# Inverse roots of the model-wide norms: square root on ScalarE and reciprocal on VectorE, in place of exp of minus half the logarithm

## What is computed

```python
def rmsnorm(x, g):
    xf = x.astype(jnp.float32)
    y = xf * lax.rsqrt(jnp.mean(xf * xf, axis=-1, keepdims=True) + EPS)
    return (y * g.astype(jnp.float32)).astype(x.dtype)

def trunk(x, c, g_norm, w_ada, b_ada, g_final, even_p, odd_p):
    for l in range(DEPTH):
        mod = jax.nn.silu(c) @ w_ada[l] + b_ada[l]
        shift, scale, gate = jnp.split(mod, 3, axis=-1)
        h = rmsnorm(x, g_norm[l]) * (1 + scale[:, None, :]) + shift[:, None, :]
        ...
        x = x + gate[:, None, :] * out
    return rmsnorm(x, g_final)
```

## Time and profile before

| | |
|---|---|
| median of 3 runs | 1512.5 us |
| lowest and highest run | 1511.76 and 1519.93 us |
| the profiled execution's own time | 1513.49 us |
| its span on the core | 1511.7 us |
| mean granted clock of TensorE | 0.995 |
| busy share PE / DVE / ACT / POOL | 97% / 56% / 45% / 24% |

### The profile page before, as it was taken

One profiled execution on the slowest core, in us unless ns is written; L12 is line 12 of the kernel. 1 busy time (PEld: TensorE's weight loads), 2 busy tenths in 40 slices (PEclk: granted clock), 3 DMA queues, 4 the chain that ended last, 5 costly groups with the idle time before them and its releaser, 6 DMA issues.

```text
span 1511.7 us, 18941 instructions
## 1 busy us (share of the span) xinstructions
PE 1463.7 (97%) x7188; PEld 1117.8 (74%) x7188; DVE 852.8 (56%) x1523; ACT 678.3 (45%) x1170; POOL 355.3 (24%) x448
## 2 busy tenths in 40 slices
PE   8999999999999999999999999999999999999996
PEld 5677765678777787878887886567867778787885
DVE  7523345755885527884443345575588651789423
ACT  3323446645433435543543344674443353555233
POOL 2011023431200023755110002342120002376311
PEclk9999999999999999999999999999999999999999
DMA  9566732224332331116234443221432333111531
GB/s 382 200 214 215 256 117 85 64 56 132 102 94 84 126 104 49 43 48 230 86 127 130 126 125 98 84 57 57 140 98 86 96 113 115 52 42 31 181 97 69
DMA packets 54618, 174.27 MB, mean 115 GB/s; under 512 B 6000, under 2 KB 7408, under 8 KB 52224
## 3 DMA queue, kind: packets, MB, share of 16 engines
q1 hardware_dynamic: 54528, 173.07, 35.7%
HBM read 149.94 MB, written 23.10 MB: 114 GB/s over the span
## 4 chain that ended last, share of the span: by engine, by line
PE 81%; DVE 8%; ACT 5%; DMA 3%; issue 2%; POOL 1%; SPq 0%; DVEq 0%; ACTq 0%; POOLq 0%
PE ps L553 21%; PE ps L554 21%; PE ps L555 21%; PE ps L1095 4%; PE ps L1130 2%; PE ps L1149 2%; PE ps L1618 1%; PE ps L1601 1%; DMA at<-w_ada 1%; DVE w_lo L535 1%; PE ps L302 1%; PE ps L1652 1%; PE ps L1441 1%; PE ps L1112 1%; DMA at<-z_kept 1%
## 5 line engine op out<-in xcount | busy, mean ns | idle before, releaser
L535 DVE TENSOR_TENSOR w_lo<-at,w_hi 128x1024 fp32r<-128x1024 f32 x160 | 199.0, 1244 | 355.2 <-ACT w_hi L523 355.2
L523 ACT ACTIVATE w_hi<-at 128x1024 fp32r<-128x1024 f32 x162 | 169.4, 1046 | 122.6 <-PE ps L555 121.1
L553 PE MATMUL ps<-h_e_hi,w_hi 128*128 128x512 f32 x480 | 190.8, 398 | 7.8 <-DVE w_lo L535 7.8
L555 PE MATMUL ps<-h_e_hi,w_lo 128*128 128x512 f32 x480 | 187.1, 390 | 0.0
L554 PE MATMUL ps<-h_e_lo,w_hi 128*128 128x512 f32 x480 | 186.9, 389 | 0.0
L553 PE MATMUL ps<-h_a_hi,w_hi 128*128 128x512 f32 x384 | 153.6, 400 | 1.8 <-DVE h_a_lo L585 1.0
L554 PE MATMUL ps<-h_a_lo,w_hi 128*128 128x512 f32 x384 | 150.2, 391 | 0.0
L555 PE MATMUL ps<-h_a_hi,w_lo 128*128 128x512 f32 x384 | 150.1, 391 | 0.0
L553 PEld LDWEIGHTS ps<-h_e_hi,w_hi 128*128 128x128 f32 x480 | 90.0, 188 | 43.7 <-DVE at L1427 11.7
L555 PEld LDWEIGHTS ps<-h_e_hi,w_lo 128*128 128x128 f32 x480 | 90.1, 188 | 19.3
L554 PEld LDWEIGHTS ps<-h_e_lo,w_hi 128*128 128x128 f32 x480 | 90.2, 188 | 18.3 <-issue 0.5
(11 more groups left out here) (289 smaller groups left out, 2972.8 us busy)
## 6 DMA issues: line engine op xcount, KB each, us to landing
at<-blocks_in SPq DMA_DIRECT2D x162, 512.0 KB, 3.7
at<-w_ada SPq DMA_DIRECT2D x32, 512.0 KB, 4.6
at<-w_ada SPq DMA_DIRECT2D x8, 1024.0 KB, 18.1
at<-xs SPq DMA_DIRECT2D x4, 2048.0 KB, 10.5
z_kept<-at SPq DMA_DIRECT2D x32, 256.0 KB, 2.2
at<-z_kept SPq DMA_DIRECT2D x32, 256.0 KB, 2.9
sg_kept<-at SPq DMA_DIRECT2D x16, 256.0 KB, 4.5
at<-sg_kept SPq DMA_DIRECT2D x16, 256.0 KB, 2.7
```

The source lines that it names most:

```text
L523: act.activation(whi[:, n % PAIRS, :, cols], wring[:, n % SLOTS, :, cols], ACT.Copy).then_inc(sem("w_hi"), 1)
L535: dve.tensor_tensor(wlo[:, n % PAIRS], wring[:, n % SLOTS], whi[:, n % PAIRS].bitcast(F32), ALU.subtract)\
L553: pe.matmul(o, stationary[0], moving[0], start=first, stop=False)
L555: return pe.matmul(o, stationary[1], moving[0], start=False, stop=final)
```

## The change

At all six places the Ln becomes a Sqrt with the same scale and bias, and the Exp is dropped. The tile then holds the root. A RECIPROCAL on DVE, in place on the same 128x512 tile, takes the Exp's part and raises the semaphore that Exp raised. The early table load asks for Sqrt's table.

```diff
         def n_rstd(act, bank):
 
-            act.preload_act_table(ACT.Ln)
+            act.preload_act_table(ACT.Sqrt)
             act.wait_ge(sem("nx_ms"), at("nx_ms", 1))
-            act.activation(rstd, ps(bank), ACT.Ln, bias=cst("eps"), scale=1.0 / D).then_inc(sem("nx_ln"), 1)
-            act.wait_ge(sem("nx_ln"), at("nx_ln", 1))
-            act.activation(rstd, rstd, ACT.Exp, scale=-0.5).then_inc(sem("rstd_done"), 1)
+            act.activation(rstd, ps(bank), ACT.Sqrt, bias=cst("eps"), scale=1.0 / D).then_inc(sem("nx_ln"), 1)
+
+        def n_inverse(dve):
+
+            dve.wait_ge(sem("nx_ln"), at("nx_ln", 1))
+            dve.reciprocal(rstd, rstd).then_inc(sem("rstd_done"), 1)
...
         def fin_scale(dve, j):
 
+            if j == 0:
+                dve.wait_ge(sem("fin_ms"), at("fin_ms", 1))
+                dve.reciprocal(y_rstd, y_rstd).then_inc(sem("fin_rs"), 1)
             dve.wait_ge(sem("fin_rs"), at("fin_rs", 1))
...
         def dve_up(dve):
             dve.wait_ge(sem("shl"), at("shl", 1))
+            dve.wait_ge(sem("ln_done"), at("ln_done", 1))
+            dve.reciprocal(rstd, rstd).then_inc(sem("rstd_done"), 1)
             dve.wait_ge(sem("rstd_done"), at("rstd_done", 2))
```

More of the change, by code:

```diff
@@ L74 @@
 Group = namedtuple("Group", "a_sync a_gpsimd a_tensor a_scalar a_vector e_sync e_gpsimd e_tensor e_scalar e_vector act_split dve_split stream_weights"
-                           " dve_h act_h n_square n_gpsimd n_tensor n_rstd fin_tensor fin_rstd fin_scale fin_out")
+                           " dve_h act_h n_square n_gpsimd n_tensor n_rstd n_inverse fin_tensor fin_rstd fin_scale fin_out")
 def out1_block(b):
@@ L454, in p_vector @@
         dve.wait_ge(sem("mod_set"), 3)
+        groups[0].n_inverse(dve)
         dve.wait_ge(sem("rstd_done"), 1)
@@ L663, in fin_rstd @@
         def fin_rstd(act, bank):
-            act.preload_act_table(ACT.Ln)
+            act.preload_act_table(ACT.Sqrt)
             act.wait_ge(sem("ms_full"), at("ms_full", 2))
-            act.activation(y_rstd, ps(bank), ACT.Ln, bias=cst("eps"), scale=1.0 / D).then_inc(sem("fin_ms"), 1)
-            act.wait_ge(sem("fin_ms"), at("fin_ms", 1))
-            act.activation(y_rstd, y_rstd, ACT.Exp, scale=-0.5).then_inc(sem("fin_rs"), 1)
+            act.activation(y_rstd, ps(bank), ACT.Sqrt, bias=cst("eps"), scale=1.0 / D).then_inc(sem("fin_ms"), 1)
         def fin_scale(dve, j):
+            if j == 0:
+                dve.wait_ge(sem("fin_ms"), at("fin_ms", 1))
+                dve.reciprocal(y_rstd, y_rstd).then_inc(sem("fin_rs"), 1)
             dve.wait_ge(sem("fin_rs"), at("fin_rs", 1))
@@ L1381, in act_up @@
         def act_up(act):
-            act.preload_act_table(ACT.Ln)
+            act.preload_act_table(ACT.Sqrt)
             act.wait_ge(sem("ms_full"), at("ms_full", 1))
-            act.activation(rstd, ps(MS_BANK), ACT.Ln, bias=cst("eps"), scale=1.0 / D).then_inc(sem("ln_done"), 1)
-            act.wait_ge(sem("ln_done"), at("ln_done", 1))
-            act.activation(rstd, rstd, ACT.Exp, scale=-0.5).then_inc(sem("rstd_done"), 1)
+            act.activation(rstd, ps(MS_BANK), ACT.Sqrt, bias=cst("eps"), scale=1.0 / D).then_inc(sem("ln_done"), 1)
             act_h(act, 1, 1, h_E, range(2))
@@ L2029, in e_vector @@
                     if n == N_AT + 3:
+                        groups[g + 1].n_inverse(dve)
                         dve.wait_ge(sem("rstd_done"), 2 * (g + 1) + 1)
@@ L2039, in group @@
         return Group(a_sync, a_gpsimd, a_tensor, a_scalar, a_vector, e_sync, e_gpsimd, e_tensor, e_scalar, e_vector, act_split, dve_split,
-                     stream_weights, dve_h, act_h, n_square, n_gpsimd, n_tensor, n_rstd, fin_tensor, fin_rstd, fin_scale, fin_out)
+                     stream_weights, dve_h, act_h, n_square, n_gpsimd, n_tensor, n_rstd, n_inverse, fin_tensor, fin_rstd, fin_scale, fin_out)
     groups.extend(group(g) for g in range(G))
```

## The result

| | before | after |
|---|---|---|
| median of 11 runs | 1513.13 us | 1527.82 us |
| lowest and highest | 1510.34 and 1521.68 us | 1519.84 and 1531.89 us |
| the profiled execution's own time | 1513.49 us | 1529.53 us |
| its span, mean granted clock | 1511.7 us, 0.995 | 1527.7 us, 0.985 |
| busy us of DVE / ACT | 852.8 / 678.3 | 872.5 / 667.3 |

The account below looks back on a forecast made before the run. The prediction held that what counts is whether PE, or the program's end, waits for the inverse root. From 1512.5 us it added 7.7 (3.38 + 3 x 1.44) and 1.7 for TensorE's clock: 1521.9 us, range 1517.0 to 1530.0.

Parts of the forecast that it names:

- What the Exp's part costs: Between Ln's end and DVE's first step: 2.05 us in layer 1, 1.97 at the end, as load, Exp and handover.
- The reciprocal, 3.35 us: Each 128x512 reciprocal on DVE takes 3.35 us, extended from pairs of narrow ones in the same setting.
- Start-up +3.38: Start-up: the reciprocal and a handover of 0.03 us are all new, since Exp and load were hidden; +3.38 us.
- Layer 1 +1.44 each: Layer 1, both groups: reciprocal and handovers take 3.49 us in place of 2.05, +1.44 us each.
- The end +1.44: End of the program: reciprocal and handovers take 3.41 us in place of 1.97, +1.44 us.
- Hidden places, 0: First group's last projection and second group's first projection: PE never stops there, so the change costs 0.
- The clock, +1.7: Layer 1, both groups: TensorE's granted clock falls behind the longer waits, 0.85 us each, +1.7 us.
- the rival in which the clock holds: Layer 1: no added clock fall, the sum without that term, +7.7 us or 1520.2 us; chance 0.25.
- Start-up clock, "no change there": Start-up: the granted clock falls already behind PE's stop, so no change was counted there.
- A longer reciprocal: Rival, every place: reciprocal takes 4.3 to 5.5 us, sum 11.5 to 16.3 us, total 1525 to 1533.3 us; chance 0.17.
- a plain pass: Rival, every place: the wide reciprocal takes only 0.67 us, sum -3.0 us, total 1509.5 us; chance 0.08.
- slack in layer 1: Rival: layer 1 has unseen slack, so only start-up and end count, +4.8 us, 1517.3 us; chance 0.08.

Follow-up runs that it names:

- e1_start: Sqrt and reciprocal only at the start-up's norm of the first group, otherwise the kernel before; ratio 1.0021 (0.9994 to 1.0048).
- e3_end: Sqrt and reciprocal only at the second group's final norm, at the very end, otherwise the kernel before; ratio 1.0001 (0.9973 to 1.0029).
- e4_hidden: Sqrt and reciprocal only at the second group's first norm and the first group's final norm, otherwise the kernel before; ratio 1.0003 (0.9978 to 1.0027).
- e8_start_fill: e1_start with nine filler matmuls on TensorE in the 4.4 us wait for the first h_lo; 1520.78 us, ratio 1.0032 to the kernel before.
- e2_layer1: Sqrt and reciprocal only at the two norms of layer 1, otherwise the kernel before; ratio 1.0029 (1.0002 to 1.0055).
- e5_one_table: Kernel before, Ln and Exp kept, early load naming the table set that holds both; 1508.68 us against 1519.19, ratio 0.9964.
- e6: Kernel before with seven filler matmuls on TensorE in the start-up phase; 1521.74 us, ratio 1.0014 (0.9990 to 1.0038).
- e7: e5_one_table with seven filler matmuls on TensorE in the start-up phase; 1518.13 us, ratio 0.9995 to the kernel before.

## Why the prediction was right, and where it was off

- **What bounds the kernel.** Right. ACT is rid of 11 us (678.3 to 667.3) and DVE does 20 us more, and neither number tells anything of the 8.3 us lost; the four places where PE or the end waits for the root tell it.
- **What the Exp's part costs.** Right: 0.69 us for the Sqrt and handovers of 0.03 to 0.1 us, as in the earlier trace rows. The Sqrt's own load is early in layer 1; at the end it stands on the path, but so did Ln's, so it cancels.
- **The reciprocal, 3.35 us.** Right to 0.01 us, from pairs of narrow ones that are two orders of size away. The choice that mattered was to take pairs in one setting rather than the means, which would have given 5.5. That it came out to 0.01 us is luck: one ns more or less in a pair's difference moves R by 0.25 us, and the first pair isn't quite in one setting (its reciprocal of 165 ns starts behind a wait of 0.94 us, the one of 178 ns a tenth of a us behind an accumulator read). The Trainium skill, *VectorE: DVE Perf Modes*, section "First, the fixed hardware budget", gives the reciprocal a repeat count of 8, and the prediction's reading of it as eight cycles for an element gave 4.3 us. The measured 6.3 ns an element are about six cycles at the 0.96 GHz of *Trainium Architecture — The Big Picture* (the Trainium skill), so the measurement decides against eight.
- **Start-up +3.38.** Measured +3.39 and +3.38 (e1_start).
- **Layer 1 +1.44 each.** Measured +1.45 in both groups and both kernels. One detail was wrong: I had the whole delay in the wait for `w_lo`, "They grow to some 2.8 us". That wait kept its 1.3 us, and the delay came ahead of it, mostly as two waits for `h_e_lo` that cost 0.65 us each.
- **The end +1.44.** Measured +1.45, alone (e3_end) and together.
- **Hidden places, 0.** Right (e4_hidden): no wait of PE grew.
- **The clock, +1.7.** This term of the sum was mis-sized, and that wrong detail may be why: a single wait of 2.8 us, which was the reason given for a fall, never came. The fall came in one group of two and made the next stretch 0.57 us longer. What was said for the rival in which the clock holds, "the wait is broken up by a few matmuls as chunks trickle in", describes what the trace shows. The measured figure lies between the two cases, 7.7 + 0.6 = 8.3 us, though the 0.6 is no larger than the scatter of the unedited stretches (the one right behind it is 0.61 us shorter in the kernel after), so how much of it reaches the end isn't shown.
- **Start-up clock, "no change there".** Nearly right for the fall at the wait: it costs nothing behind the longer wait (e8_start_fill), and 0.5 us in the one trace of the kernel before. What the prediction missed is the other fall, between 13 and 37 us, which needs no change at all. The three times shown for the kernel before were 1511.76, 1512.5 and 1519.93: the third had the answer in it, and I took the median of the other level. The median of after (1527.82) lies 5.9 us above 1521.9 because six of its eleven runs had that fall; its runs without it have a median of 1520.5, 1.4 us below the forecast. Which of the two levels that median lands on was chance: with one run fewer in the slower group it would have been 1520.9. That 1527.82 lies in the predicted range is owed to the range's width, which was meant for a longer reciprocal, and not to anything foreseen of this fall.
- **The rivals.** A longer reciprocal, a plain pass and slack in layer 1 are excluded by 3.35 us and by e2_layer1. The reading of the table load at 2.66 us for each switch (the Trainium skill, *ScalarE: Activation LUTs*, section "What ACT_TABLE_LOAD costs") would have made the sum 3.6 us; the measured 8.3, the 1.45 us at the end (e3_end) and e5_one_table speak against it.

So the change is slower because on a 128x512 tile DVE's reciprocal takes 3.35 us, where the Exp with its load took 1.9, and at the start-up the Exp and load were hidden while DVE's time was not.

## What to carry to other kernels

An inverse root on a whole tile, where all partitions hold the same numbers, was cheapest, of the three forms that ran here, as Ln and Exp under one table set: naming the set that holds both took 1.1 to 1.3 us from each place where its load was waited for and made the kernel 0.36% faster (0.1 to 0.6). Before work is moved from one engine to another, cost the operation on the new engine at its real width (two narrow ones in the same setting give a slope) and ask at each place which of the two engines the next wait ends on. When the times of an unchanged kernel fall into two levels, find out first which level each profile belongs to, and compare stretches of the traces rather than medians of a few runs.

## What the runs showed of the hardware

- A RECIPROCAL of 512 fp32 elements on each of 128 partitions took 3345 to 3354 ns in the six kernels that have it, and one of 2 elements 155 to 166 ns in the mean. The wide one takes five times as long as a copy of the same size (672 ns).
- TensorE's granted clock fell from 1.00 to 0.50 in the midst of the start-up and stayed there for 20 to 24 us, in five of the ten profiled executions. In the kernel after PE had been busy for all of the 5.03 us ahead of the fall; in e6 and e7 a wait of 1.51 and 1.30 us lies there. A group of eight matmuls of the modulation took 1.88 us in place of 1.04. By their times about half of all runs have the fall (from two of ten in e3_end to seven of ten in e2_layer1), and they are some 8 us longer.
- Filler matmuls in the place of the wait of 4.4 us kept the clock at 1.00 (e8_start_fill), where it fell with the wait (e1_start), while others earlier in the start-up didn't prevent the fall that comes there (e6, e7).
- The same sequence of short waits in layer 1 (0.48, 0.49 and 1.3 us) was followed by a fall of the clock in one group and not in the other, in both kernels that had it.
- 3.4 us of the lower clock cost the first two projection blocks 0.5 us when they began 1.5 us behind the first matmul (the kernel before), and nothing when they began with it, at the end of a fall that had set in during the wait (e1_start).
